# Rotating queries and keys with row copies by DMA in place of a permutation by TensorE

## The reference

```python
t1 = t[..., :half]              # half = 8
t2 = t[..., half:ROPE_DIM]      # ROPE_DIM = 16
return jnp.concatenate([t1 * c - t2 * s, t2 * c + t1 * s, t[..., ROPE_DIM:]], axis=-1)
```

## Time and profile before

| | |
|---|---|
| median of three runs | 2448.69 us (2448.49 to 2450.82) |
| the profiled execution, its own time | 2449.95 us |
| its span, first to last instruction | 2447.9 us |
| PE busy | 2386.8 us, 98% |
| DVE busy | 1906.9 us, 78% |
| POOL busy | 1178.2 us, 48% |
| ACT busy | 1098.3 us, 45% |
| granted PE clock, mean | 0.989 |

### The profile page before, as it was taken

One profiled execution on the slowest core, in us unless ns is written; L12 is line 12 of the kernel. 1 busy time (PEld: TensorE's weight loads), 2 busy tenths in 40 slices (PEclk: granted clock), 3 DMA queues, 4 the chain that ended last, 5 costly groups with the idle time before them and its releaser, 6 DMA issues.

```text
span 2447.9 us, 31946 instructions
## 1 busy us (share of the span) xinstructions
PE 2386.8 (98%) x11378; PEld 1953.2 (80%) x11378; DVE 1906.9 (78%) x2456; ACT 1098.3 (45%) x1885; POOL 1178.2 (48%) x798
## 2 busy tenths in 40 slices
PE   9999999999989999999999999999998999999998
PEld 7777788878768888878877878887876888788886
DVE  6777757673699787779979966778289888899976
ACT  6454656562543333344336436555163333544423
POOL 4666542211555555555545463431256555555552
PEclk9999999999999999999999999999998999999998
DMA  4311321232113232355332872223213444654522
GB/s 164 78 54 51 88 61 40 60 116 71 56 48 129 86 112 96 120 177 159 113 94 81 189 171 61 60 60 109 76 57 130 169 144 149 215 181 138 181 78 103
DMA packets 233260, 264.64 MB, mean 108 GB/s; under 512 B 18448, under 2 KB 145168, under 8 KB 232976
## 3 DMA queue, kind: packets, MB, share of 16 engines
q1 hardware_dynamic: 229504, 250.29, 32.5%
q0 software_dynamic: 3168, 11.54, 2.5%
q10 hardware_dynamic: 432, 0.79, 0.1%
HBM read 170.53 MB, written 61.60 MB: 95 GB/s over the span
## 4 chain that ended last, share of the span: by engine, by line
PE 84%; DVE 8%; POOL 3%; ACT 2%; issue 2%; DMA 1%; SPq 0%; POOLq 0%; DVEq 0%; ACTq 0%
PE PS L1768 24%; PE PS L1773 23%; PE PS L1770 23%; PE PS L1866 3%; PE PS L1853 2%; PE PS L1887 2%; PE PS L1884 2%; PE PS L1847 2%; DVE R0f L2173 1%; PE PS L1850 1%; DVE R L2180 1%; POOL stage L2650 0%; DVE R L2249 0%; PE PS L1852 0%; DVE X L2257 0%
## 5 line engine op out<-in xcount | busy, mean ns | idle before, releaser
L1768 PE MATMUL PS<-R,wh 128*128 128x512 f32 x2860 | 1137.4, 398 | 23.3 <-DVE stage L2161 10.8
L2626 POOL TENSOR_TENSOR lows<-values,wh 128x512 fp32r<-128x512 f32 (+2 forms) x483 | 717.5, 1490 | 890.0 <-ACT wh L2378 679.1
L1773 PE MATMUL PS<-R,wh 128*128 128x512 f32 x2860 | 1122.0, 392 | 8.7 <-DVE R L2180 5.9
L1770 PE MATMUL PS<-R,lows 128*128 128x512 f32 x2496 | 977.4, 392 | 1.2 <-POOL lows L2626 1.2
L1768 PEld LDWEIGHTS PS<-R,wh 128*128 128x128 f32 x2860 | 541.2, 189 | 137.8 <-DVE stage L2161 12.7
L1773 PEld LDWEIGHTS PS<-R,wh 128*128 128x128 f32 x2860 | 540.0, 189 | 129.4 <-DVE R L2180 7.1
L2378 ACT ACTIVATE wh<-values 128x512 fp32r<-128x512 f32 (+2 forms) x484 | 299.3, 618 | 580.6 <-PE PS L1773 552.3
L1770 PEld LDWEIGHTS PS<-R,lows 128*128 128x128 f32 x2496 | 471.4, 189 | 93.4 <-issue 3.8
L2257 DVE TENSOR_TENSOR X<-PS,X 128x1024 f32<-128x1024 f32 x168 | 204.2, 1217 | 35.8 <-PE PS L1773 35.3
L2626 POOL TENSOR_TENSOR late_r<-late,wh 128x512 fp32r<-128x512 f32 (+1 forms) x92 | 137.2, 1492 | 113.8 <-DVE values L2155 65.6
L2161 DVE TENSOR_TENSOR stage<-PS,stage 128x512 f32<-128x512 f32 x156 | 105.5, 685 | 64.5 <-PE PS L1773 64.3
(11 more groups left out here) (277 smaller groups left out, 3091.0 us busy)
## 6 DMA issues: line engine op xcount, KB each, us to landing
scr_hid<-R1f SPq DMA_DIRECT2D x177, 256.0 KB, 3.0
R0f<-scr_hid SPq DMA_DIRECT2D x92, 256.0 KB, 3.6
values<-w_in_dram SPq DMA_DIRECT2D x88, 256.0 KB, 2.8
R1f<-scr_hid SPq DMA_DIRECT2D x85, 256.0 KB, 3.3
values<-w_ff_dram SPq DMA_DIRECT2D x62, 256.0 KB, 3.0
values<-w_ff_dram SPq DMA_DIRECT2D x100, 128.0 KB, 2.4
R<-R SPq DMA_DIRECT2D x96, 128.0 KB, 2.3
X<-X POOLq DMA_DIRECT2D x22, 512.0 KB, 5.6
```

The costliest lines, as they stand in the source:

```text
L1768: e.matmul(PS[:, b, :], wh, high, start=s["start"], stop=False, skip_group_check=on)
L1770: e.matmul(PS[:, b, :], wl, high, start=False, stop=False, skip_group_check=on)
L1773: m = e.matmul(PS[:, b, :], wh, low, start=False, stop=s["stop"], skip_group_check=on)
L2626: e.tensor_tensor(T.wl[piece.v][:, 0:m], T.wv[piece.v][:, 0:m], T.wh[:, piece.h, 0:m].bitcast(F), ALU.subtract).then_inc(*sg.up("w_lo", pi ...
```

## The change

The permutation matrix and its 16 matmuls are gone. In their place SP issues six copies for each rotated half: rows 8 to 15 to rows 0 to 7, rows 0 to 7 to 8 to 15, rows 16 to 63 as they are, and the same in the lower half of the partitions, all from the first stage to the second. DVE multiplies the second stage with the sines in place. The waits for the second stage to be free pass from DVE to SP. DVE and POOL wait for the last of the six copies; two semaphores (`partner0`, `partner1`) take turns, and SP does not start a set before the sine product of the set two before it is done.

```diff
             def rotate(half, i, which=which, split=split):
-                b, given = self.side_bank()
                 j, gj = self.next_stage()
                 key = (u.name, which, half)
-                self.step("rotate", key=key, half=half, i=i, j=j, gj=gj, b=b, given=given)
+                partner = f"partner{self.rotations % 2}"
+                self.rotations += 1
+                self.step("partner", key=key, i=i, j=j, gj=gj, partner=partner, given=self.partner_read[partner])
+                self.step("rotate", key=key, half=half, i=i, j=j, partner=partner)
                 self.step("rotate_add", key=key, i=i, j=j)
-                self.bank_given[b] = [("rot_sin", key)]
+                self.partner_read[partner] = [("rot_sin", key)]
                 self.stage_given[j] = [("rot", key)]
...
-            e.matmul(PS[:, s["b"], :], T.perm[:, :], T.stage[s["i"]], start=True, stop=True).then_inc(*sg.up("permuted", s["key"]))
...
         elif kind == "rotate":
-            for event in s["gj"]:
-                w.wait_ge(*sg.at(*event))
             w.wait_ge(*sg.at("table", 0))
-            w.wait_ge(*sg.at("permuted", s["key"]))
-            e.tensor_tensor(stage[s["j"]], PS[:, s["b"], :], T.TABF[:, 1, cols(s["half"])], ALU.mult).then_inc(*sg.up("rot_sin", s["key"]))
+            w.wait_ge(*sg.at(s["partner"], s["key"]))
+            e.tensor_tensor(stage[s["j"]], stage[s["j"]], T.TABF[:, 1, cols(s["half"])], ALU.mult).then_inc(*sg.up("rot_sin", s["key"]))
...
+        elif kind == "partner":
+            key, st, to = s["key"], stage[s["i"]], stage[s["j"]]
+            for event in s["gj"] + s["given"]:
+                w.wait_ge(*sg.at(*event))
+            w.wait_ge(*sg.at("evac", key))
+            for n, (a, b, rows) in enumerate(((0, 8, 8), (8, 0, 8), (16, 16, 48), (64, 72, 8), (72, 64, 8), (80, 80, 48))):
+                e.dma_start(to[a:a + rows, :], st[b:b + rows, :]).then_inc(*sg.up(s["partner"], key if n == 5 else (key, n), by=16))
```

More of the change, by code:

```diff
@@ L25 @@
 NV = 129
-C_ID, C_PERM, C_COS, C_SIN, C_SEL, C_MASK = 0, 128, 256, 1280, 2304, 3328
+C_ID, C_COS, C_SIN, C_SEL, C_MASK = 0, 128, 1152, 2176, 3200
 NC = C_MASK + 3 * 512
@@ L175, in __init__ @@
         self.ones = self.new("ones", [128, 128], F, 512)
-        self.perm = self.new("perm", [128, 128], F, 512)
         self.maskb = self.new("maskb", [128, 128], BF, 256)
@@ L300, in __init__ @@
         self.on_slot = {}
+        self.rotations, self.partner_read = 0, dict(partner0=[], partner1=[])
         self.fetches, self.fetched = 0, {f"fetched{i // 2}{i % 2}": [] for i in range(4)}
@@ L1820, in tensor_program @@
             m.then_inc(*sg.up("rs_sum", (s["n"], half)))
-        elif kind == "rotate":
-            for event in s["given"]:
-                w.wait_ge(*sg.at(*event))
-            w.wait_ge(*sg.at("evac", s["key"]))
-            w.wait_ge(*sg.at("perm", 0))
-            e.matmul(PS[:, s["b"], :], T.perm[:, :], T.stage[s["i"]], start=True, stop=True).then_inc(*sg.up("permuted", s["key"]))
         elif kind == "by_tokens":
@@ L2630, in gpsimd_program @@
             w.wait_ge(*sg.at("table", 0))
-            w.wait_ge(*sg.at("permuted", key))
+            w.wait_ge(*sg.at(s["partner"], key))
             e.tensor_tensor(st, st, T.TABF[:, 0, cols(s["half"])], ALU.mult).then_inc(*sg.up("rot_cos", key))
@@ L2708, in sync_program @@
             e.dma_start(T.ident[:, :], cst[:, C_ID:C_ID + 128]).then_inc(*sg.up("ident", 0, by=16))
-            e.dma_start(T.perm[:, :], cst[:, C_PERM:C_PERM + 128]).then_inc(*sg.up("perm", 0, by=16))
         elif kind == "x_load":
@@ L2996, in constants @@
         for j in range(8):
-            c[o + j + 8, C_PERM + o + j] = 1.0
-            c[o + j, C_PERM + o + j + 8] = 1.0
             c[o + j, C_COS:C_COS + S] = cos[j]
```

1 line of the change is left out of this document (removed).

## The result

The changed kernel takes 2473.62 us (median of 4 runs, 2471.57 to 2475.45); the kernel before took 2448.59 us beside it (4 runs, 2446.56 to 2450.82). The ratio is 1.0102, 95% interval 1.0088 to 1.0116: slower by 1.0%, clear of the noise. The prediction had the direction and a third of the size. The profiled execution took 2471.57 us, its span is 2469.8.

What follows compares the result with a forecast made beforehand. It saw a full PE beside a chain through POOL, the change relieving the first and lengthening the second. 10.3 - 7.0 + 5 = 8.3 us on 2449.95 gave 2458 (2457 on the median), range 2445 to 2466.

Steps and rivals of the forecast that it cites:

- -7.0: From a1's second half to a3: the same work remains less eight permutations on PE, -7.0 us.
- +5: From a1's second half to a3: uncovered stalls at DVE, PE's value transpose and unit starts, +5 us, bounds 0 and 12.
- a0's scores: First unit: POOL's longer serial chain and the key copies start the scores at 86.5 in place of 77.2, +9.3 us.
- SP's two issues 1.2 and the landing 2.2 give 86.4: First unit's end: after POOL's last low part at 83.0, the last key copies issue and land by 86.4.
- PE's 23 steps at 0.68 us: First unit: behind the second value evacuation's wait to 69.9, PE has 23 steps of 0.68 us, ending at 86.2.
- a1's scores: Second unit: late key halves start the scores at 129.8 in place of 115.0, +14.8 us.
- 37.8 us: a0's attention: DVE is full, so its length stays 37.8 us, putting a1's scores at 124.3 at the earliest.
- The second group: a1's next group of scores: 120 steps done in both kernels, at 141.3 against 131.0, +10.3 us.
- PE's relief: Rival: PE's saved time passes through, the end 14 us earlier at 2435, or 2442 if only behind a1; chance 0.13.
- The price of a copy: Each set of six copies: 0.65 us an issue, 3.9 us of SP, 6.1 us to landing, where the permutation took 0.9.
- The sine product: DVE's product now reads two SBUF tiles beside POOL: 0.69 to 1.15 us each; three in DVE's full stretch, +0.5 us taken.
- SP becomes the bound: Rival: sets wait at SP's queue head or copies land one after another, giving 2465 to 2475; chance 0.11.

Runs made afterwards that it cites:

- one_copy: The changed kernel, same order, with one copy of 128 rows for each set of six (partner rows not exchanged, other numbers computed): 2471.2 us.
- filled_waits: The changed kernel, same order, with matmuls of ones by ones put into PE's waits in the first unit and the last group's end: 2481.1 us.
- short_permutation: The kernel before, with each permutation matmul covering 128 of its 512 columns (output incomplete): 2449.8 us.
- work_put_back: The changed kernel, same order, with four matmuls of ones (0.88 us) ahead of each of twelve query and key halves of a1 to a3: 2478.0 us.
- true_costs: The changed kernel, laid out anew with the copies' bytes and SP issue time corrected in the planner's table: 2461.6 us.
- old_order_one_copy: The kernel before's order, with one copy of 128 rows per rotated half in place of the permutation (partner rows not exchanged): 2452.4 us.

## Why the prediction was off

The forecast was +8.3 us on the profiled execution; `b0` came 23.2 us late and the end 21.6 (25.0 by the medians). Of the 14.9 us that are missing at `b0`, 4.9 arose ahead of `a0`'s scores, 2.7 in `a0`'s attention, -0.8 up to the second group and 8.1 behind it. The step that failed by most is the last: "-7.0" for eight permutations with "+5" for new stalls gave -2.0, and 6.1 us more were needed. The chain ahead of it was right, within 1.6 us, up to POOL's last low part, and wrong in SP's queue and in PE's order. The terms against the traces, at the prediction's own marks:

- **a0's scores, +9.3 foretold, +14.2 found.** The mechanism held: fifth rest part first, cosine at 56.6, four halves in a row (POOL done at 84.55 for 83.0), and PE's wait of 8.9 us at the second value transpose to 70.1 (foretold 69.9). Of the miss of 4.9, POOL made 1.6. The step that failed is "SP's two issues 1.2 and the landing 2.2 give 86.4": it let the last copies go out at once, and left 3.4 us from POOL's end to the landing; it took 6.3. SP was behind with `a1`'s first set, the copies waited 2.0 us, and the second landed 3.8 us behind its issue. With one copy a set that piece shrank by 3.5 us (one_copy), of which 2.6 arrived.
- **PE's 23 steps at 0.68 us** took 17.7 us (70.82 to 88.54, by starts) for 15.6: the first 4 us of them ran at half clock. Hidden here, as filled_waits shows.
- **a1's scores, +14.8 foretold, +22.4 found.** "Scores at 129.8" followed the keys. They were not what the scores waited for, which the prediction itself had named as a sign of being wrong. "37.8 us", 124.3 at the earliest, was taken from the kernel before, in which all transposes of `a0`'s last group stand behind `a1`'s first scores; in the new order of PE the first go of them and two steps stand ahead. The step went by DVE's and POOL's order and left PE's out: with the 41.7 us that the first go needed before, and `a0`'s true start, it would have come to 133.1 for this go, which ran at 133.91; then 3.5 us at half clock to 137.36. DVE is busy for 41.65 us of the now 46.0 (35.59 of 38.0 before), so it is nearly full in both.
- **The second group, +10.3 foretold, +17.1 found**: the same miss less 0.8.
- **"-7.0 us" for eight permutations and "+5 us" for new stalls, -2.0 together; found +6.1** (182.4 for 176.3 us). This is the largest miss, 8.1 us. The 14 steps more ahead of the third unit's scores are there, as foretold (174 for 160), and those scores come 17.4 us later behind the mark; the two units behind it take 11.3 us less. By the windows, PE's busy time fell by only 2.6 us (165.0 for 167.6) and its idle time grew by 8.7 (17.4 for 8.7). The "+5" was worked out from a wait for a set and the value transpose behind it. By the waits of PE from 148.1 to 330.5 us, no wait was for a set or a key copy directly: 6.5 us were for ACT's exponential (L2471), 5.7 for DVE's normalisation (L2064), 2.1 for DVE's split (L2099), 1.3 for evacuations. The first term took PE's relief at face value. By short_permutation it is worth nothing in the old order, by work_put_back about 5 in the new. With the latter, the new stalls are some 11 us, inside the upper bound of 12 that was given; with the former, 6. Which split is right stays open, since no run changed only one of the two in one order. That the stalls' 5 us were too few, by either, is shown.
- **The price of a copy.** 0.65 us an issue and 3.9 a set on SP were right (0.627; 3.9). The 6.1 to landing are some 0.5 too many: rows 7 count the 2.2 us from the start of an issue, and the prediction counted them from its end. **The sine product**, taken with +0.5 us in `a0`'s attention and bounded by 1.15 us each: five of the 16 lie above that bound. The seven longer ones add 3.7 us over 0.69 each, 2.6 of it ahead of `a0`'s scores, where nothing was counted. The Trainium skill (GPSIMD Engine Reference, section 1, Specifications) has GpSimd share its SBUF interface with VectorE, with contention where an instruction of the latter has two SBUF inputs. The trace agrees: all longer ones lie beside POOL's products. Not every sine product pays, as the prediction read it, but those that begin inside one of POOL's. In DVE's full stretch that was one of three, 0.5 us, so the term came out right there.
- **The rivals.** PE's relief did not pass (short_permutation). "SP becomes the bound", 2465 to 2475, holds the measured time, and the queue did hold `a0` from 77.8 to 87.6; but with one copy in place of six the end moved by 2.4 us, so SP is not what holds the kernel, and the number is hit by luck. What part the order has, true_costs shows: laid out with the sets' true costs, 12 of the 25 us come back. What remains is not taken apart. In the old order even one copy, which lands 2.3 us behind its issue, leaves `b0` 10 to 11 us late, where a permutation takes 0.9.

What stays open is how far each fall of the clock behind 148 us cost time by itself, and how much of the 11.6 us by which true_costs is late at `b0` is latency and how much order: the same kernel in another order was 16.2 late.

## What to carry to other kernels

Work that is taken off the fullest engine is worth what the next waits leave of it: before counting a relief, shorten that work in the old kernel and see. When a table of assumed durations lays out the order, a new kind of step needs its true cost in the table before the idea is judged; here the wrong entries cost a third to a half of the loss (7 to 12 of 23 us at `b0`). And when the end moves by a few microseconds, change an unrelated entry of the table once, to see how far the end moves by luck; judge the change at the last mark of the stretch that it touches, by more than one execution. And read the order of every engine around the mark that is forecast, the fullest one first: here one set of transposes that had moved ahead of the scores made the forecast's duration that of something else.

## What the runs showed of the hardware

- PE idle for 9 us was followed by half clock for the next 5 us of work, and waits of 2.7 us in a stretch with little work had falls behind them too (88.7 to 91.4 idle, 92 to 96 at half clock). The Trainium skill (TensorE: Matmul & The Clock Gate, Part 1) has the clock drop when the engine is not kept busy; the trace agrees. Filling the two waits ahead of `a0`'s scores kept the clock at 1.00 up to 128 us and gained no time.
- An issue of these copies on SP took 0.627 us in the median (0.542 to 1.589), whether for 8 rows or 48, and 0.48 us for one of 128 rows. The Trainium skill (DMA: Bandwidth & Descriptors, Rules for kernel authors) advises to merge small transfers; in the old order the trace agrees, 28 us earlier at `b0` with one copy than with six (old_order_one_copy); in the new order merging gained nothing there (one_copy). The cost in the old order is the queue's time, by which the last copy lands later, since six copies and one move the same 128 rows.
- A product of DVE that reads two tiles of SBUF and a product of POOL did not run side by side: whichever began second took longer. A sine product that began inside one of POOL's ended 0.55 us behind its end, in all seven cases (0.72 to 1.80 us long in place of 0.69); the one that began first kept its 0.68 us, and POOL's took 1.53 for 1.27.
